# Down projection of a Strassen-like feed-forward layer: weight operands prepared beside gate/up, kept in DRAM, and products that share banks

## The reference: what is computed

```python
def swiglu(h, w_gu, w_down):
    gu = h @ w_gu
    gate, up = jnp.split(gu, 2, axis=-1)
    return (jax.nn.silu(gate) * up) @ w_down

def reference(x, ...):
    for l in range(DEPTH):          # DEPTH = 2
        h = rms_norm(x, attn_norm[l])
        x = x + hybrid_mixer(h, w_in[l], qk_gain[l], rpb[l], sink[l], out_gain[l], w_out[l])
        h = rms_norm(x, ffn_norm[l])
        x = x + swiglu(h, w_gu[l], w_down[l])    # w_gu[l]: 1024 x 5632, w_down[l]: 2816 x 1024
    return x
```

## Time and profile before

| | us |
|---|---|
| median of 3 runs | 2795.83 (2792.17 to 2801.12) |
| profiled execution, its time | 2790.08 |
| profiled execution, span | 2788.4 |
| TensorE busy | 2626.0 (94%) |
| VectorE busy | 1748.1 (63%) |
| ScalarE busy | 1063.9 (38%) |
| GpSimd busy | 810.3 (29%) |
| mean granted TensorE clock | 0.983 |

### The profile page before, as it was taken

The page is one execution under the profiler, slowest core; times in us unless marked ns, Lnnn a source line. Parts: engine busy times, 40 slices in busy tenths (PEclk is TensorE's granted clock), DMA queues, the critical chain, the costliest instruction groups (busy, mean ns, idle before and its releaser), DMA issues. The chain is left out here.

```text
span 2788.4 us, 37901 instructions
## 1 busy us (share of the span) xinstructions
PE 2626.0 (94%) x12976; PEld 2154.8 (77%) x12976; DVE 1748.1 (63%) x3180; ACT 1063.9 (38%) x2098; POOL 810.3 (29%) x675
## 2 busy tenths in 40 slices
PE   5999999989799999999979999999897999999997
PEld 5877787778688888777678778878686888887775
DVE  4277667672655555599944776666626555557997
ACT  3222655552522222334342226555525222223332
POOL 2000221110155444446400003111002544545553
PEclk9999999999899999999989999999998999999999
DMA  5211610013122222522232116000221222226023
GB/s 164 82 39 38 148 42 19 12 42 107 61 91 91 83 68 61 199 81 87 65 125 64 38 46 155 25 13 12 96 77 59 91 84 79 73 61 264 12 90 110
DMA packets 230942, 219.84 MB, mean 79 GB/s; under 512 B 54768, under 2 KB 191984, under 8 KB 230768
## 3 DMA queue, kind: packets, MB, share of 16 engines
q1 hardware_dynamic: 222864, 217.61, 24.5%
q10 hardware_dynamic: 7904, 0.04, 0.2%
HBM read 171.87 MB, written 45.73 MB: 78 GB/s over the span
## 5 line engine op out<-in xcount | busy, mean ns | idle before, releaser
L1996 PE MATMUL psum<-OPH_t,WH 128*128 128x512 f32 x704 | 274.6, 390 | 6.8 <-DVE WL L1531 4.9
L1996 PE MATMUL psum<-OPH_t,WL 128*128 128x512 f32 x704 | 274.0, 389 | 0.0
L1996 PE MATMUL psum<-OPL_t,WH 128*128 128x512 f32 x704 | 273.9, 389 | 0.0
L1804 PE MATMUL psum<-BH,AH 128*128 128x512 f32 x616 | 247.2, 401 | 19.8 <-DVE BL L1587 19.0
L1531 DVE TENSOR_TENSOR WL<-RAW,WH 128x512 fp32r<-128x512 f32 x132 | 160.7, 1217 | 157.1 <-ACT WH L1073 157.1
L958 ACT ACTIVATE T<-T,G 128x192 f32<-128x192 f32 (+4 forms) x352 | 176.7, 502 | 194.2 <-DVE G L1284 190.6
L1805 PE MATMUL psum<-BL,AH 128*128 128x512 f32 x616 | 241.2, 392 | 0.0
L1806 PE MATMUL psum<-BH,AL 128*128 128x512 f32 x616 | 241.0, 391 | 0.0
L1996 PE MATMUL psum<-OPH_b,WH 128*128 128x512 f32 x528 | 208.9, 396 | 15.6 <-DVE WL L1531 8.5
L1894 PE MATMUL psum<-QK,QS 128*128 (+5 forms) x576 | 214.4, 463 | 2.0 <-DVE G L1284 2.0
L1420 DVE COPY PT<-psum 128x256 f32<-128x256 f32 (+3 forms) x254 | 105.3, 415 | 174.6 <-PE psum L1910 173.7
(11 more groups left out here) (194 smaller groups left out, 5937.9 us busy)
## 6 DMA issues: line engine op xcount, KB each, us to landing
RAW<-in_w_gu SPq DMA_DIRECT2D x176, 256.0 KB, 3.8
WDS<-in_w_down SPq DMA_DIRECT2D x88, 256.0 KB, 2.6
UR<-in_w_in SPq DMA_DIRECT2D x56, 256.0 KB, 3.2
g_mid<-GRES SPq DMA_DIRECT2D x28, 512.0 KB, 2.6
WDK<-in_w_down SPq DMA_DIRECT2D x44, 256.0 KB, 6.0
x_res<-X SPq DMA_DIRECT2D x2, 4096.0 KB, 13.4
PR<-in_w_out SPq DMA_DIRECT2D x32, 256.0 KB, 4.3
X<-x_res SPq DMA_DIRECT2D x2, 4096.0 KB, 14.4
```

What stands on the lines that cost most here:

```text
L1804: t.matmul(dst, sh, mh, start=start, stop=False)
L1996: last = t.matmul(dst[:, :], w[i][:, k, :], h[o][:, k, :], start=(i in (1, 5, 6) and k == 0 and part == 0), stop=(i in (2, 3, 4) and k == ...
```

## The change

The B operands of the down projection are made during gate/up. Beside products 14 to 147 of gate/up (`MADE_AT`), 77 parts are made one after the other in two buffers BP: GpSimd sums two quarters where the part is a sum (`part_added`, two products ahead), ScalarE copies the high half (`part_high`), VectorE subtracts the low half (`part_low`), SP stores both halves to DRAM as one piece of 512 KB (`part_away`). The raw tiles of a pair k lie in one buffer RAWD of 16 KB per partition, which is loaded anew when the seventh part of the pair before is done. In the down projection a step loads its part into one of eight slots BR (`part_in`), and ScalarE and VectorE only prepare A. SP's order there is: parts 0 to 3 when all parts are stored, 4 to 7 after product (6, 21), the tiles of g, x, then part 8 and on, each when step n-8 is done.

For room, 4 tiles of g stay in SBUF instead of 8, so 18 go out and come back. GpSimd's sums of gate/up weights are spread over the products (`weight_sums(j + 1, which)`) where they stood in one piece behind `gated(j)`. The order of products is 3 and 5 interleaved (3 with a lead of three steps), then 4, 1, 7, 6, 2. Product 7 adds onto the banks of 4 and product 6 onto those of 1 (no start flag), after these have been added to one target; so 1 and 4 have one target less in `M`. Additions stand one step later in VectorE's order (LAST_STEP + 4).

Removed lines are cut to a few below; gone with them are WDK, WDS, SUMB, BH, BL, `b_part`, `b_source` and VectorE's `step_sum`.

```diff
-    G_KEPT = 8
+    G_KEPT = 4
     G_SENT = NCH - G_KEPT
     g_mid = dram("g_mid", (G_SENT, P, S))
...
+        RAWD = at_kb("RAWD", [P, 2, 2, 512], F32, 200)
+        BP = at_kb("BP", [P, 2, 2, 512], F32R, 208)
...
+        BR = [at_kb(f"BR{i}", [P, 2, 512], F32R, (200 if i < 4 else 4) + 4 * i) for i in range(8)]
...
+        GL = [at_kb(f"GL{i}", [P, S], F32, (44 + 4 * i) if i < 10 else 152 + 4 * (i - 10)) for i in range(G_SENT)]
...
-            M = {1: (((0, 0), 1, (1, 1)), ((0, 0), 1, (1, 1)), ((0, 0, 1), (1, 1, 1))),
+            M = {1: (((0, 0), 1, (1, 1)), ((0, 0), 1, (1, 1)), ((0, 0, 1),)),
-                 4: (((1, 1), 0, None), ((1, 0), -1, (0, 0)), ((0, 0, 1), (1, 0, 1))),
+                 4: (((1, 1), 0, None), ((1, 0), -1, (0, 0)), ((1, 0, 1),)),
...
+            PAIRS = [(G_SENT + 2 * k, G_SENT + 2 * k + 1) for k in range(2)] + [(2 * k, 2 * k + 1) for k in range(9)]
-            STEPS = [(m, k) for k in range(NK) for m in (2, 5)] + [(m, k) for m in (1, 3, 4, 7, 6) for k in range(NK)]
-            RUNS = [2, 5, 1, 3, 4, 7, 6]
...
+            LEAD = 3
+            STEPS = [(3, k) for k in range(LEAD)]
+            for k in range(NK):
+                STEPS += [(5, k)] + ([(3, k + LEAD)] if k + LEAD < NK else [])
+            STEPS += [(m, k) for m in (4, 1, 7, 6, 2) for k in range(NK)]
+            RUNS = [3, 5, 4, 1, 7, 6, 2]
             LAST_STEP = {m: max(n for n, st in enumerate(STEPS) if st[0] == m) for m in M}
...
             BANKS = {m: ((0, 1, 2, 6), (7, 3, 4, 5))[RUNS.index(m) % 2] for m in M}
+            PARTS = (2, 5, 1, 3, 4, 6, 7)
+            MADE_AT = {q: 14 + 134 * q // (7 * NK) for q in range(7 * NK)}
+            MADE_BESIDE = {n: [q for q in MADE_AT if MADE_AT[q] == n] for n in range(-2, PRODUCTS)}
...
+            def part_source(q):
+                first, sign, second = M[PARTS[q % 7]][1]
+                return BP[:, q % 2, 1, :].bitcast(F32) if sign else raw_part(first)
...
                 def down_tiles(k):
+                    if k:
+                        sp.wait_ge(part_lo, 7 * k)
...
-                        sp.dma_start(WDK[:, k, i, :], w_down[bass.ds(l, 1), at_:at_ + P, 512 * i:512 * i + 512]
...
+                        sp.dma_start(RAWD[:, i, :, :], w_down[bass.ds(l, 1), at_:at_ + P, :]
+                                     .rearrange("a p (h n) -> p (a h) n", h=2)).then_inc(rawd_in, 16)
+                def g_out(j):
+                    sp.wait_ge(g_s, 2 * j + 2)
+                    sp.dma_start(g_mid[j], GRES[:, j % G_KEPT, :]).then_inc(g_sent[j % G_KEPT], 16)
+                def part_away(q):
+                    sp.wait_ge(part_lo, q + 1)
+                    sp.dma_start(w_parts[q], BP[:, q % 2, :, :].bitcast(F32)).then_inc(part_out[q % 2], 16)
+                    if q % 7 == 6 and q // 7 + 1 < NK:
+                        down_tiles(q // 7 + 1)
+                sp.wait_ge(op_lo, 7)
+                down_tiles(0)
+                for n in range(PRODUCTS):
+                    i, j = ORDER[n]
+                    if i == 3 and j + 2 < NCH:
+                        raw_tiles(j + 2)
+                    for q in MADE_BESIDE[n - 1]:
+                        part_away(q)
+                    if n >= 2 and ORDER[n - 2][0] == 3 and ORDER[n - 2][1] < G_SENT:
+                        g_out(ORDER[n - 2][1])
+                def part_in(n):
+                    if n >= 8:
+                        sp.wait_ge(step_s, n - 7)
+                    m, k = STEPS[n]
+                    sp.dma_start(BR[n % 8][:, :, :].bitcast(F32), w_parts[part_no(m, k)]).then_inc(b_in[n % 8], 16)
                 def g_back_in(j):
...
+                for i in range(2):
+                    sp.wait_ge(part_out[i], 16 * ((7 * NK + 1 - i) // 2))
+                for i in range(G_KEPT):
+                    sp.wait_ge(g_sent[i], 16 * len(range(i, G_SENT, G_KEPT)))
+                for n in range(4):
+                    part_in(n)
...
+                for n in range(4, 8):
+                    part_in(n)
+                for i, js in ((5, range(0, 2)), (2, range(2, 6)), (7, range(6, 10)), (4, range(10, 14)), (3, range(14, 18))):
+                    sp.wait_ge(product, DONE[i, NCH - 1])
+                    for j in js:
+                        g_back_in(j)
...
-                for m in (4, 0):
+                for m in (0, 4):
...
+                for n in range(8, len(STEPS)):
+                    part_in(n)
...
+                def part_high(q):
+                    sign = M[PARTS[q % 7]][1][1]
+                    if sign:
+                        act.wait_ge(part_sum, sums_of_parts(q))
+                    else:
+                        act.wait_ge(rawd_in, 32 * (q // 7 + 1))
+                        if q >= 2:
+                            act.wait_ge(part_out[q % 2], 16 * (q // 2))
+                    a.activation(BP[:, q % 2, 0, :], part_source(q), ACT.Copy).then_inc(part_hi, 1)
                 def step_hi(n):
...
+                    if n in SUM_NO:
+                        act.wait_ge(sum_pool, SUM_NO[n] + 1)
...
-                    a.activation(BH[:, n % 4, :], b_source(n), ACT.Copy).then_inc(ab_hi, 1)
+                        tile_, half = M[m][0][0]
+                        if k < 2:
+                            act.wait_ge(g_s, 2 * PAIRS[k][tile_] + half + 1)
+                        else:
+                            act.wait_ge(g_got[k - 2], 32)
+                    a.activation(AH[:, n % 4, :], a_source(n), ACT.Copy).then_inc(a_hi, 1)
...
+                    for q in MADE_BESIDE[n]:
+                        part_high(q)
...
-                    v.tensor_tensor(SUMB[:, n % 2, :], b_part(n, 0), b_part(n, 2), ALU.add).then_inc(sum_dve, 1)
+                def part_low(q):
+                    dve.wait_ge(part_hi, q + 1)
+                    v.tensor_tensor(BP[:, q % 2, 1, :], part_source(q), BP[:, q % 2, 0, :].bitcast(F32),
+                                    ALU.subtract).then_inc(part_lo, 1)
                 def step_lo(n):
...
-                    v.tensor_tensor(BL[:, n % 4, :], b_source(n), BH[:, n % 4, :].bitcast(F32), ALU.subtract).then_inc(ab_lo, 1)
+                    dve.wait_ge(a_hi, n + 1)
+                    v.tensor_tensor(AL[:, n % 4, :], a_source(n), AH[:, n % 4, :].bitcast(F32), ALU.subtract).then_inc(a_lo, 1)
                 def add_product(m):
+                    if m != RUNS[0]:
+                        dve.wait_ge(x_sum, 4 * RUNS.index(m))
...
+                    for q in MADE_BESIDE[n]:
+                        part_low(q)
...
                 for n in range(2, len(STEPS)):
...
+                    for m in RUNS[:-1]:
+                        if n == LAST_STEP[m] + 4:
+                            if m == RUNS[0]:
+                                dve.wait_ge(x_again, 32)
-                add_product(6)
+                add_product(RUNS[-1])
...
+                def part_added(q):
+                    first, sign, second = M[PARTS[q % 7]][1]
+                    if sign:
+                        pool.wait_ge(rawd_in, 32 * (q // 7 + 1))
+                        if q >= 2:
+                            pool.wait_ge(part_out[q % 2], 16 * (q // 2))
+                        g.tensor_tensor(BP[:, q % 2, 1, :].bitcast(F32), raw_part(first), raw_part(second),
+                                        ALU.add if sign > 0 else ALU.subtract).then_inc(part_sum, 1)
                 def step_sum(n):
...
+                    c = SUM_NO[n]
+                    if c < 4:
+                        pool.wait_ge(product, DONE[5, NCH - 1])
...
+                        pool.wait_ge(a_lo, SUM_STEPS[c - 4] + 1)
+                    if k >= 2:
+                        pool.wait_ge(g_got[k - 2], 32)
+                    g.tensor_tensor(SUMA[:, c % 4, :], a_part(n, 0), a_part(n, 2),
+                                    ALU.add if M[m][0][1] > 0 else ALU.subtract).then_inc(sum_pool, 1)
...
+                for n, (i, j) in enumerate(ORDER):
+                    for q in MADE_BESIDE.get(n + 2, ()):
+                        part_added(q)
+                    if 0 < j < NCH - 1:
+                        weight_sums(j + 1, {5: (5, 6), 7: (7,), 3: (3,)}.get(i, ()))
+                    if i == 3:
+                        if j == NCH - 1:
+                            pool.wait_ge(g_s, 2 * j)
+                            step_sum(SUM_STEPS[0])
+                        gated(j)
...
+                for n in SUM_STEPS[1:]:
...
                 def down_step(n):
...
+                    pe.wait_ge(a_lo, n + 1)
+                    pe.wait_ge(b_in[n % 8], 16 * (n // 8 + 1))
...
-                                     BH[:, n % 4, :], BL[:, n % 4, :], k == 0, k == NK - 1)
+                                     BR[n % 8][:, 0, :], BR[n % 8][:, 1, :], k == 0 and m not in (6, 7),
+                                     k == NK - 1 and m not in (1, 4), skip=True)
...
```

## The result

The changed kernel takes **2885.2 us** (median of 4 runs, 2882.1 to 2889.3) against 2796.1 for the kernel before (4 runs): a ratio of 1.032, 95% interval 1.030 to 1.034. It is 89 us slower; the forecast was 2798.8, with 2777 to 2829 as its range. The profiled execution took 2882.1 us, its span 2880.4.

A forecast was written before the change was run, and what follows sets the result against it. TensorE was taken to bound gate/up, VectorE and GpSimd in turn to slow down's steps. Per layer, -5.5 for down and tail plus 7 for gate/up gave +1.5, for two layers +3.0: 2798.8 us, range 2777 to 2829.

The forecast's parts named there:

- What down saves: Down projection: removing BH, BL and SUMB ends TensorE's slow steps and dry spells, saving 19.0 us per layer.
- The stall at step 8: Down projection: TensorE waits for part 8, loaded behind g and X; 9.1 us per layer (7.6 to 12.6).
- rival D: Change to down: the load burst runs at the skill's 358 GB/s, landing 6 us later; 2811 us, chance 0.05.
- The clock: Down projection, after the stall at step 8: matmuls at the lower clock level cost 2.0 us per layer.
- The tail: End of a layer: the last product has 8 additions instead of 4, nothing beside them; plus 2.4 us per layer.
- Turn-taking: Gate/up: two-input work of VectorE and GpSimd in turn fills 17.4 of 19.04 us per chunk; costs 2 us per layer.
- Rival B: Gate/up: VectorE and GpSimd in turn become the bound; 2818 to 2837 us, middle 2827, chance 0.22.
- Rival A: Gate/up absorbs all the added work, 0 to 2 us per layer instead of 7; 2787 us, chance 0.24.
- rival C: Down: part loads don't wait behind g and X, or step 8 isn't short; 11.1 us per layer saved, 2777, chance 0.07.
- The raw tiles: Gate/up, changes of pair: waiting for the next raw tiles costs 2.5 + 2.5 and 0.3 for each other eight, 7.4 us.
- The stores themselves hold nothing up.: Gate/up: part_out is wanted two parts (9.4 us) later and 204 GB/s is half the full rate, so stores cost nothing.
- Together 7, less than additive.: Gate/up: turn-taking and raw-tile waits together cost 7 us per layer (0 to 20), as a stalled TensorE lets VectorE catch up.

The follow-up runs named there:

- e1: The changed kernel with X loaded behind part 15 instead of ahead of part 8; 2866.0 us (one run).
- e8: The changed kernel with w_down's raw tiles loaded for the first pair only and only the first two parts stored; 2783.0 us profiled.
- e6: The changed kernel with w_down's raw tiles loaded for the first pair only and without GpSimd's sums of parts; 2787.3 us profiled.
- e2: The changed kernel with w_down's raw tiles loaded for the first pair only and all parts made from them; 2804.6 us profiled.
- e5: The changed kernel with only the first two parts stored, the others made but not stored; 2833.1 us profiled.
- e3: The changed kernel without GpSimd's sums of parts, each part split from one raw tile; 2820.9 us profiled.
- e15: The changed kernel with GpSimd's sum of a part placed behind its weight sums and g tiles of the same product; 2858.0 us, ratio 1.0235.
- e7: The changed kernel with a second raw-tile buffer loaded one pair ahead, 2 g tiles kept instead of 4, X behind part 15; 2793.9 us, ratio 1.0003.
- e16: e7 with GpSimd's part sum behind its weight sums and g tiles, and parts 8 to 11 loaded between g tiles 16 to 19; 2774.1 us, ratio 0.993.
- e13: e7 with w_gu loads issued from ScalarE's queue and parts 8 to 11 loaded between g tiles 16 to 19; 2803.8 us, ratio 1.004.

## Why the prediction was wrong

Point by point, by its own steps, per layer.

1. **What down saves (19.0).** Right. Slow steps are gone; e1 with its stall removed takes 210.1 where 209.4 is the bound, 18.3 saved.
2. **The stall at step 8 (9.1, 7.6 to 12.6).** Right in place, cause and size: 10.7. The burst was issued 15.9 us ahead of down's first matmul instead of 16.6, and took 48.4 us to the landing of part 8 where 46.4 had been reckoned. e1 shows the cause. The Trainium skill's 358 GB/s (DMA: Bandwidth & Descriptors, section Bandwidth), which it gives where both cores of an HBM stream, would have made it 15. With one core running here the trace has 410 GB/s in that stretch, and rival D falls.
3. **The clock (2.0).** 2.9: it stayed at the lower level until 1253.4. A term 0.9 too small.
4. **The tail (2.4).** Right: 4.87 for eight, +2.3 and +2.4.
Together -2.8 per layer where -5.5 stood: 5.4 us of the miss for both layers.
5. **Turn-taking (2).** That two-input work of VectorE and GpSimd runs in turn is visible (a subtraction of 1.77 us where 0.68 would do, 960.57, beside GpSimd's sum at 960.06), and its price in gate/up by itself is 1.3 or less (e8; e6, with the stores and without the sums, 0.4). The Trainium skill, SBUF — State Buffer, section Who interferes with whom, says that a VectorE instruction with two SBUF inputs contends with a GpSimd instruction that reads SBUF; the trace agrees. Rival B, that this is the bound, falls with e8, though the measured time lies on its side and beyond it: its time would have been closer for a reason that isn't the one found. Rival A falls by the 48.6 us added to gate/up, rival C by the stall.
6. **The raw tiles (7.4).** Here the prediction failed. The mechanism was named, and the time from the part's end to its raw tiles was near (5.6 reckoned, 6.2 measured). The step that failed is "the seventh part is done 2.0 us into its product": it was done 6.3 us in (first matmul at 956.01, the part's end at 962.34). Its sum stood behind GpSimd's other work, its Copy waited for the sum, and its subtraction stood behind U2 and two splits of weights. Turn-taking had its part in this: the five subtractions that VectorE made from 954.17 to 962.34 took 4.5 us more than at 0.68 each, which costs nothing in e8, where no reload hangs on them. 4 us later at a change of pair turn the "0.3 for each of the other eight", for which two products of room had been reckoned, into stalls of 2 to 4 us, and the two tight ones from 2.5 into 6 to 7. Without the reload gate/up adds 7.6 instead of 48.6 (e2). A second term had been put at nothing without a reason: the clock behind such stalls. The prediction priced it for step 8 only; in gate/up it took 13 of the 50 us of layer 1.
7. **"The stores themselves hold nothing up."** Wrong: 22 us of the 49 go with them (e5). This is not all the buffer's wait, since the raw tiles, with no store ahead of them, land sooner as well (median 4.3 us instead of 5.3); how the 22 us divide is open. The step compared a mean need (two parts, 9.4 us) with a landing of 2.6. But GpSimd asks two products ahead of ScalarE, so that a buffer is held from its sum to its landing, and beside 1 MB of w_gu the landing can be 6.7 (its median is 2.8). The half-used mean rate, 204 GB/s, told nothing of it.
8. **"Together 7, less than additive."** Wrong in sign. The sums and stores without the reload add 7.6 us (e2), the reload and stores without the sums 19.0 (e3), all of them 48.6. The costs feed each other; the reading that fits the trace is this: the late store holds GpSimd's sum, the sum holds ScalarE's Copy, this makes the seventh part late and so the raw tiles, and while all stand, weight sums, g tiles and splits queue up. The prediction priced each wait as if all else were on time. Without the reload 7.6 us are left, without the stores 26.4, without both 1.3: most of the 48.6 needs both. e15 eases the loop on GpSimd's side (-16), e7 on the reload's (-34).

What stays open is how e16's last 5 us per layer of gate/up split between the stores' landing and the added work.

## What to carry to other kernels

Before work is put beside a full engine, write down the whole cycle of a shared buffer (filled, read by each engine, stored, free) with every operation that stands in line ahead of each step, and compare it with the time until it is wanted; a mean rate or a mean busy share does not show it. Ask which reader of a buffer is the last, since it need not be the last step of the work (here waiting for it alone was not tried), and price the lower clock behind every stall, not only behind the longest. In an in-order engine put an operation that may wait for a transfer behind what others need, not ahead: here that order alone was worth 23 to 27 us. Ask for the next operand while one is still in hand; a second pair of raw tiles and X behind part 15, paid with two more g tiles on their way out and back, took the 89 us away (e7), and with the order on GpSimd and four parts between g tiles (e16) made the change 0.7% faster than the kernel before.

## What the runs showed of the hardware

A 512 KB store from SBUF, 2.6 us at best, took 6.6 and 6.7 us when 1 MB of loads in rows of 512 bytes had been issued 3.3 us before it, and in these two cases it made no difference whether the loads were on the same queue (e7) or on another one (e13). Through the burst at the change to down the DMA queues carried 397 to 419 GB/s in the changed kernel (1205 to 1255 us) and 399 to 408 in the kernel before (1160 to 1195), one core running. After 10.7 us of idleness matmul starts were 0.43 us apart for 5.7 us (1247.72 to 1253.40), then 0.23.
